# Attention row sums: inverse broadcast through DRAM in place of TensorE, and an earlier first transpose for short tiles

## The reference, cut to what matters

```python
s = jnp.einsum('bqhd,bkhd->bhqk', q[:, q0:kend], k[:, :kend]) * scale
s = s + c[:, :, q0:kend, None] - c[:, :, None, :kend]
p = jax.nn.softmax(jnp.where(mask[None, None], s, NEG_INF), axis=-1)
outs.append(jnp.einsum('bhqk,bkhd->bqhd', p, v[:, :kend]))
```

## Time and profile before

| what | value |
|---|---|
| median of three runs | 2929.63 us |
| the profiled execution (its span, the one time that the profile gives for it) | 2924.8 us |
| TensorE matmul busy | 2840.5 us, 97% |
| VectorE busy | 1712.9 us, 59% |
| ScalarE busy | 616.3 us, 21% |
| GpSimd busy | 1350.4 us, 46% |
| mean granted TensorE clock | 0.993 |

### The profile page before, as it was taken

The page is one execution under the profiler, slowest core; times in us unless marked ns, Lnnn a source line. Parts: engine busy times, 40 slices in busy tenths (PEclk is TensorE's granted clock), DMA queues, the critical chain, the costliest instruction groups (busy, mean ns, idle before and its releaser), DMA issues.

```text
span 2924.8 us, 40628 instructions
## 1 busy us (share of the span) xinstructions
PE 2840.5 (97%) x14442; PEld 2069.8 (71%) x14442; DVE 1712.9 (59%) x4617; ACT 616.3 (21%) x1269; POOL 1350.4 (46%) x1140
## 2 busy tenths in 40 slices
PE   8999999999999999998999989999999999999997
PEld 4478888888875555554455767878877777777775
DVE  6665656656346767674677534777677773332326
ACT  2221212110025454552110100011111111111114
POOL 3433534447730110101355335677667666555645
PEclk9999999999999999999999999999999999999999
DMA  6500110101121103014435456889989989999986
GB/s 219 184 6 1 31 45 1 30 15 44 30 77 35 63 30 129 28 33 170 173 137 159 131 198 197 270 277 277 271 277 289 291 271 302 305 304 305 317 258 254
DMA packets 192571, 470.49 MB, mean 161 GB/s; under 512 B 27384, under 2 KB 108104, under 8 KB 166632
## 3 DMA queue, kind: packets, MB, share of 16 engines
q1 hardware_dynamic: 145424, 347.63, 33.3%
q0 software_dynamic: 44640, 111.84, 16.5%
q10 hardware_dynamic: 2304, 8.39, 0.7%
HBM read 349.64 MB, written 118.11 MB: 160 GB/s over the span
## 4 chain that ended last, share of the span: by engine, by line
PE 39%; DMA 6%; DVE 3%; POOL 2%; issue 2%; SPq 1%; another core or an unknown queue 0%; ACT 0%; DVEq 0%; POOLq 0%; ACTq 0%
PE ps L3021 18%; PE ps L2796 6%; DMA moe_xg<-t_rows,index 5%; PE ps L2969 4%; PE ps L2940 3%; PE ps L2852 2%; DVE moe_xT L2097 2%; PE ps L2937 2%; POOL moe_xg L2523 1%; PE ps L2862 1%; PE ps L2815 1%; POOL moe_fin L2605 1%; PE ps L2806 0%; DMA base_rows<-moe_yo,index 0%
## 5 line engine op out<-in xcount | busy, mean ns | idle before, releaser
L2523 POOL DMA_INDIRECT moe_xg<-t_rows,index x433 | 428.6, 990 | 174.7 <-issue 139.2
L3021 PEld LDWEIGHTS ps<-moe_xT,moe_wg 128*128 128x128 f32 x2048 | 352.5, 196 | 54.6 <-issue 31.3
L3021 PE MATMUL ps<-moe_xT,moe_wg 128*128 128x192 f32 (+22 forms) x2048 | 380.0, 338 | 9.3 <-DVE moe_hh L1997 5.4
L3021 PE MATMUL ps<-moe_xT,moe_wu 128*128 128x192 f32 (+22 forms) x2048 | 376.3, 337 | 0.0
L3021 PEld LDWEIGHTS ps<-moe_xT,moe_wu 128*128 128x128 f32 x2048 | 354.2, 197 | 4.8
L2544 POOL DMA_INDIRECT base_rows<-moe_yo,index x100 | 231.0, 2310 | 273.2 <-DVE moe_yo L2111 116.8
L2097 DVE STREAM_TRANSPOSE moe_xT<-moe_xg 128x256 f32<-128x256 f32 x433 | 235.1, 610 | 174.2 <-DMA moe_xg<-t_rows,index 155.9
L1296 POOL TENSOR_TENSOR fox_diag<-fox_c,fox_causal 128x128 f32<-128x128 f32 x128 | 55.8, 457 | 450.9 <-DVE fox_mx L1325 446.1
L2660 ACT ACTIVATE moe_sl<-ps 128x256 f32<-128x256 f32 (+19 forms) x144 | 49.6, 345 | 953.9 <-PE ps L3021 736.8
L1997 DVE TENSOR_TENSOR moe_hh<-moe_sl,ps 128x256 f32<-128x256 f32 (+19 forms) x144 | 49.7, 358 | 292.4 <-ACT moe_sl L2660 194.9
L1319 DVE CUSTOM_DVE_ANT_0 hT<-ps,fox_c 128x512 f32<-128x512 f32 (+7 forms) x320 | 166.3, 560 | 63.0 <-PE ps L1581 62.7
(11 more groups left out here) (373 smaller groups left out, 5052.1 us busy)
## 6 DMA issues: line engine op xcount, KB each, us to landing
moe_wg<-in_we_gate SPq DMA_DIRECT2D x64, 1024.0 KB
moe_wu<-in_we_up SPq DMA_DIRECT2D x64, 1024.0 KB
moe_wd<-in_we_down SPq DMA_DIRECT2D x64, 1024.0 KB
fox_c<-ck SPq DMA_DIRECT2D x8, 1032.0 KB, 8.9
emb_xin<-in_x SPq DMA_DIRECT2D x16, 512.0 KB, 3.9
h_rows<-emb_hr SPq DMA_DIRECT2D x16, 512.0 KB, 2.7
ret_w<-in_w_in SPq DMA_DIRECT2D x16, 512.0 KB, 6.6
moe_yt<-h_rows SPq DMA_DIRECT2D x16, 512.0 KB
```

Source lines behind the costliest of these rows:

```text
L2523: pool.indirect_dma_start(out=xg[g % NXG][:, :], out_offset=None, in_=quarters, in_offset=bass.IndirectOffsetOnAxis(ap=route.index4[:, AT4 ...
L3021: ins = pe.matmul(out, w[:, c, f:FF:FC], xT[u][:, c, 0:n], start=(c == 0), stop=(c == DC - 1))
```

## The change

What it does, part by part:

1. `scatter` and its ones matrix are gone, as are the four diagonal matrices of `inverse` and the PSUM copy `keep`.
2. In their place SyncE runs `inverse_rows(n)`: it waits for the reciprocal, stores the 128 x 4 values to a small DRAM buffer, transposed (r outside, query inside, single elements of 4 bytes), waits for that store to land, and loads them back twice, once per head, broadcast over 64 partitions, into `rB` (256 columns).
3. `finish(n)` on VectorE now waits for the weighing of the whole tile and for both loads.
4. The store of tile n - 1 to `foxT` is issued after `inverse_rows(n)`, and the loads of pair p + 1 come after the store of the last tile of pair p - 1, in the middle of tile 8 (16) in place of its beginning.
5. `early` holds for t > 0 in place of t > 2, so for t = 2 and t = 1 too. For t = 1 the first two score chunks of tile n + 2 move with the transposes, in front of the last weighing.

```diff
-        onesf = sb("onesf", [P, FD])
-        rd = [sb(f"rd{b}", [P, 4, P]) for b in range(2)]
+            def inverse_rows(n):
+                b = n % 2
+                sp.wait_ge(inverted, n + 1)
+                sp.dma_start(rinv_rows[b].rearrange("r k -> k r"), rinv[b][:, :], allow_slow_non_contiguous=True).then_inc(rinv_out, 16)
+                sp.wait_ge(rinv_out, 16 * (n + 1))
+                if n >= 2:
+                    sp.wait_ge(scaled, n - 1)
+                for a in range(2):
+                    sp.dma_start(rB[b][FD * a:FD * (a + 1), :].rearrange("p (q k) -> p q k", q=2),
+                                 rinv_rows[b].rearrange("(q a) k -> a q k", a=2)[a].partition_broadcast(FD)).then_inc(rB_in[b], 16)
+
+            def store(n):
+                p, t = order[n]
+                sp.wait_ge(scaled, n + 1)
+                sp.dma_start(foxT[2 * FD * p:2 * FD * (p + 1), QT * t:QT * (t + 1)], oT[n % 2][:, :]).then_inc(o_s[n % 2], 16)
+
             for n, (p, t) in enumerate(order):
+                inverse_rows(n)
                 if n in TURN_AT:
...
-                sp.wait_ge(scaled, n + 1)
-                sp.dma_start(foxT[2 * FD * p:2 * FD * (p + 1), QT * t:QT * (t + 1)], oT[n % 2][:, :]).then_inc(o_s[n % 2], 16)
-                if (n + 1) % TILES == 0 and p + 2 < PAIRS:
-                    pair_values(p + 2)
-                    pair_gates(p + 2)
+                if n >= 1:
+                    store(n - 1)
+                if n >= 1 and n % TILES == 0 and p + 1 < PAIRS:
+                    pair_values(p + 1)
+                    pair_gates(p + 1)
+            store(NT - 1)
...
-                    dve.wait_ge(spread, n - 1)
+                    dve.wait_ge(rinv_out, 16 * (n - 1))
                 dve.reciprocal(rinv[b][:, :], rs[b][:, :]).then_inc(inverted, 1)
-                dve.wait_ge(inverted, n + 1)
-                for r in range(4):
-                    ins = dve.tensor_scalar(rd[b][:, r, :], ident[:, :], rinv[b][:, r:r + 1], None, ALU.mult)
-                ins.then_inc(rd_set, 1)
...
-                dve.wait_ge(spread_c, n + 1)
+                dve.wait_ge(weighed, step0[n + 1])
+                dve.wait_ge(rB_in[b], 32 * (n // 2 + 1))
...
-            def keep(n):
...
-            def scatter(n):
...
-                early = rounds > lead[n] and order[n][1] > 2
+                early = rounds > lead[n] and order[n][1] > 0
+                ahead_of = range(first[n + 2]) if n + 2 < NT and order[n][1] else []
...
                     if early and i == rounds - 1:
+                        for u in ahead_of:
+                            scores(n + 2, u)
                         for s in after:
                             turn(n + 1, s)
...
-                if early:
-                    scatter(n)
-                else:
-                    if order[n][1] == 0:
-                        for s in after:
-                            turn(n + 1, s)
-                        scatter(n)
-                    else:
-                        scatter(n)
-                        for u in (range(first[n + 2]) if n + 2 < NT else []):
-                            scores(n + 2, u)
-                        for s in after:
-                            turn(n + 1, s)
+                if not early:
+                    for u in ahead_of:
+                        scores(n + 2, u)
+                    for s in after:
+                        turn(n + 1, s)
```

More of the change, by code:

```diff
@@ L1104, in retention_phase, with fox_phase @@
         yield
-def fox_phase(nc, ps, ident, hT, square, w_in, w_out, v_rows, ck, mixed, mT_rows, foxT, ahead):
+def fox_phase(nc, ps, ident, hT, square, w_in, w_out, v_rows, ck, mixed, mT_rows, foxT, rinv_rows, ahead):
     with Phase(nc, "fox") as ph:
@@ L1190, in fox_phase @@
         zero = lambda name: ph.zero_sems(name, 1)[0]
-        tab, ones_set = ahead.fox_tab, zero("ones_set")
+        tab = ahead.fox_tab
         w_s, v_s, c_s = ahead.fox_w, ahead.fox_v, ahead.fox_c
@@ L1203, in fox_phase @@
         turned, pT_a, pT_d, weighed = (zero(n) for n in ("turned", "pT_a", "pT_d", "weighed"))
-        inverted, rd_set, spread, spread_c, scaled = (zero(n) for n in ("inverted", "rd_set", "spread", "spread_c", "scaled"))
+        inverted, rinv_out, scaled = (zero(n) for n in ("inverted", "rinv_out", "scaled"))
+        rB_in = ph.zero_sems("rB_in", 2)
         block = yield
@@ L1284, in _ @@
                     fox_token_sum(pool, ahead, hT, g, part)
-            pool.memset(onesf[:, :], 1.0).then_inc(ones_set, 1)
             pool.wait_ge(tab, 16)
@@ L1516, in _ @@
                         exps(n + 1, q, a)
-                    if i == 0 and n >= 1:
-                        keep(n - 1)
-            keep(NT - 1)
         @block.tensor
@@ L3075, in build @@
     mixed, foxT = dram("mixed", (SEQ, RH * RD)), dram("foxT", (FH * FD, SEQ))
-    mT_rows = dram("mT_rows", (NX, P, RH * P))
+    mT_rows, rinv_rows = dram("mT_rows", (NX, P, RH * P)), dram("rinv_rows", (2, 4, P))
     t_rows, base_rows = dram("t_rows", (SEQ + SPARE, D)), dram("base_rows", (SEQ + SPARE, D))
@@ L3086, in build @@
                   retention_phase(nc, ps, ident, hT, a["square"], a["w_in"], a["retc"], v_rows, ck, mixed, ahead),
-                  fox_phase(nc, ps, ident, hT, a["square"], a["w_in"], a["w_out"], v_rows, ck, mixed, mT_rows, foxT, ahead)]
+                  fox_phase(nc, ps, ident, hT, a["square"], a["w_in"], a["w_out"], v_rows, ck, mixed, mT_rows, foxT, rinv_rows, ahead)]
         for stage in stages:
```

## The result

The changed kernel takes 2960.74 us (median of 4 runs, 2959.97 to 2971.22), the kernel before 2928.45 (4 runs, 2926.21 to 2930.67). The ratio is 1.0114, with a 95% interval from 1.0094 to 1.0134: 32.3 us more, outside the range.

The account below looks back on a forecast made before the run. It took TensorE to set the pace in the attention stretch. Gains of 8.2 + 1.2 = 9.4 us by the last tile, less 1.1 us at the end, gave 2929.6 - 8.3 = 2921.3 us, range 2917 to 2928.5.

Parts of the forecast that it names:

- The failed step: SyncE's store of the inverse sums to DRAM, 512 pieces of 4 bytes: lands in 2.3 us, bounds 1.9 and 10.2.
- the chain: Reciprocal to `rB` through DRAM: store 2.3, loads 0.4 + 2.0, three handovers of 0.05, 4.9 us; ends 4.0 and 21.
- Rival B: Expensive 4-byte store: the chain outlasts its cover and VectorE stops in `finish`; at 15 us, 2939; chance 0.06.
- SyncE's work, off the path while it lands before `finish`: The added way through DRAM: hidden in 31 tiles at 4.9 us, with 8 us over; shortest cover 13.1 us.
- Moved on SyncE: Stores and loads queued behind `inverse_rows`, and small transfers behind bulk loads, still arrive in time: cost nothing.
- rival A: The scatter's gain is taken up by longer waits in following rounds: 2928.5 to 2930.7, say 2929; chance 0.19.
- The 20 long transitions: Tiles t = 7 to 3: removing the scatter gains 0.41 us of 0.54 at each, 8.2 us.
- t = 2 and t = 1: Short-tile transitions: gain 0 at t = 2, where TensorE waits for ScalarE; 0.4 us at three t = 1, 1.2 us.
- t = 0: Four transitions where TensorE waits 0.49 us for VectorE's copy: removing the scatter lengthens the wait, gain 0.
- Rival D: Earlier transposes at t = 1 and 2 hold up a ready weighing: up to 0.3 us in seven places, 2923.4; chance 0.08.
- VectorE's diagonals: Removing 28.0 us of diagonal matrices on VectorE gains nothing, as they never stand before the copy releasing TensorE.
- The end of the stage: Last tile, without cover: `finish` and everything behind the barrier come 1.1 us later, from 0.2 to 17 by the bounds.

Follow-up runs that it names:

- experiment 3: Changed kernel with the inverse sums stored as 128 side-by-side pieces of 16 bytes, wrong output: 2922.63 us, ratio 0.9978 to the kernel before.
- 5: Changed kernel with the same 512 4-byte stores, each word 64 bytes apart, wrong output: 458.40 us from first to last reciprocal; total 3204.68 us not comparable.
- experiment 4: Changed kernel with no store or loads of the inverse sums, `rB` filled once, wrong output: 2919.4 us, ratio 0.9972 to the kernel before.
- experiment 10: Changed kernel with TensorE transposing the sums, four 512-byte rows stored, scatter in the last two tiles, old short-tile order: 2917.89 us, ratio 0.9966 to the kernel before.
- experiment 7: Kernel before with only the new order for t = 2 and t = 1, scatter kept: 2917.35 us against 2914.11, ratio 1.0009.
- 9: Changed kernel with TensorE transposing the sums, four 512-byte rows stored, scatter in the last two tiles, new order: 2909.1 us against 2914.11, ratio 0.9978.
- experiment 1: Not the kernel: single small SyncE transfers, each waited for before the next; the changed kernel's store took 9.5 to 10.1 us from issue to issue.

## Why the prediction was wrong

**The failed step** is one term of the chain: "First transfer: 2 KB, but 512 pieces of 4 bytes; I take 2.3, near the small store, with bounds 1.9 and 10.2." It measured 8.2 us for the first, 8.5 in the median and up to 16 behind bulk loads. The upper bound held the first two; the choice "near the small store" was wrong, because the store of the earlier trace rows writes pieces of 1 KB, and this one writes 16 single words into each 64 bytes, from 16 partitions. With one block in place of single words (3) the term is 1.4 us for the first and 1.9 in the median, with the same 512 single words 64 bytes apart (5) 2.5 in the median, and in both the stalls in the middle are gone.

For this step the prediction cites the Trainium skill's "DMA: Bandwidth & Descriptors", which has one descriptor per element for a non-contiguous last dimension ("Rules for kernel authors") and a read-modify-write below 512 bytes ("Specifications"). Both hold for the fast layouts as well as for the slow one, and 512 elements of 4 bytes land in 1.9 us when 16 words apart, so neither tells the two apart. Whether a read-modify-write is what makes neighbours slow no run shows.

**The rest of the chain** was nearly right: one load alone takes 2.6 to 2.9 us with its issue, and the two together 3.4 us from the first issue to `finish` in the last tile (2.4 taken). With the store in one block the last `finish` comes 5.75 us behind the reciprocal, where 4.9 was forecast.

**Rival B** was the mechanism and its chance of 0.06 too small. But its pricing was off as well: at a chain of 12 us (8.5 + 3.4 and the handovers) it gives about 2928 (7.1 us more at the end than forecast), and 2961 was measured. Three parts were missing. First, "SyncE's work, off the path while it lands before `finish`" looked at one tile; SyncE waits 9 us per tile for the landing, and in that time neither the store for the next tile nor anything else is issued. In the last two tiles the landings add up: 20.56 us in place of 12. Second, "Moved on SyncE" comes to "Nothing": the retention rows come late (11.1 us in seven waits), and tiles 19 and 20 pay, where the small transfer stands behind 4 MB. With a landing of 2 us "nothing" is right, as experiment 3 shows; the two errors are one. Third, the clock: it halved in the 6.3 us stall of tile 20.

**Its sums.** Two are a little off besides: the gain is used up at a chain of 13.2 us, not 12.9 (1.1 + 8.3 = 9.4), and rival A begins at 2927.6, not 2928.5 (a third of 9.4, less 1.1). The range ended at 2928.5, although the prediction's own bounds for the end went to 17 us.

The Trainium skill's "DMA: Bandwidth & Descriptors", section "Queues, rings and completion order", has it that an issuing engine's queue is one ring on each of the same 16 DMA engines, and that each of them takes its descriptors in ring order. The 9.8 us of the store in one block behind 3 MB, against 1.4 alone, agree.

**The gains of TensorE.** Forecast 9.4 us by the last reciprocal, measured 7.6 in 3, 4, 5 and 10.

- *The 20 long transitions*: 0.41 us each forecast, 0.32 measured (tile periods 21.33 to 21.01, 18.87 to 18.55, 16.01 to 15.69, 13.11 to 12.79 and 10.91 to 10.59, each the same in every undisturbed kernel): 6.4 instead of 8.2. The timeline of the changed kernel at the transition of the earlier trace rows:

```profile
954.18 1.04 PE L1604 MATMUL ps<-ident,hT 128*16 128x128 f32 x8 [0.76 <-ACT hT L1489]
...
955.15 0.44 PE L1629 MATMUL ps<-fox_pT,fox_v 128*64 128x128 f32 x4
955.26 0.69 DVE L1366 COPY fox_pT<-ps 128x512 f32<-128x512 f32 x1 [2.54 <-PE ps L1604]
955.52 1.20 PE L1604 MATMUL ps<-ident,hT 128*128 128x128 f32 x8
```

Step 2 starts 0.37 us behind the last weighing (0.3 to 0.4 forecast, 0.81 before). Then steps 2 and 3 take 1.20 us together instead of 1.09, which is 0.11 in the copy's wait: of 0.44 us won 0.33 is left. The mechanism is the one forecast: step 3's first matmul, first row, starts 0.14 us behind the end of VectorE's copy and 0.94 behind the last weighing (0.95 forecast). What was off is its start before, second row:

```profile
956.09 0.30 PE L1604 MATMUL ps<-ident,hT 128*128 128x128 f32 x1
955.20 0.38 PE L1600 MATMUL ps<-ident,hT 128*128 128x128 f32 x2
```

The prediction took 955.26, half of the 1.09 us behind 954.71; but the matmuls overlap, so half of a row's length is more than the distance of its starts.

- *t = 2 and t = 1*: 0 + 0.4 forecast for what lies in the period of the t = 0 tile; it is 0.65 (8.23 to 7.58). The wait for ScalarE at t = 2 is 1.50 us, where "about 0.8" was to show it: most of the 0.81 us that is gone in front of that wait came back in it. *t = 0*: 0 forecast, and the period of the t = 7 tile behind it grows by 0.3 (33.43 to 33.73). VectorE's bias for the longest tile is the bound there; TensorE arrives sooner and waits longer (the first row is the changed kernel's, against 0.49 us of idle time before):

```profile
986.08 1.22 PE L1609 MATMUL ps<-ident,hT 128*128 128x128 f32 x8 [1.08 <-DVE fox_pT L1366]
```

Rival A is right in this one place: part of what is won at t = 1 is given back at the next t = 7. Net it is 0.35 us in each of three pairs, near the 0.4. Rival D's cost exists as well, but smaller than its price: the new order alone costs a net 0.4 us at a change of pair (experiment 7), and with the scatter gone it is neutral (experiment 10 has the same 7.6 us without it).

- *VectorE's diagonals* at nothing: right for the tile periods, since 3 and 4 gain no more than the scatter's share.

**The end of the stage**: +1.1 us forecast. In experiment 3, where the chain is as forecast, the end costs 1.8; in the changed kernel 16.6. **The sum** by the forecast's own method would be -7.6 + 1.8 = -5.8, which is what experiment 3's stage shows (468.43 - 474.24). Its runs have -5.9, but with other work possible behind the stage that agreement proves little.

## What to carry to other kernels

A chain through DRAM is priced by its address pattern, not by its bytes: ask of each store whether neighbouring words are written one by one, from one partition each, and if so transpose on chip first and store long rows. (A store in one block that is read back with a stride of 4-byte elements was not run.) Where that transpose stands counts too: in 9 and 10 it stood at the end of the tile and used up the cover in the t = 2 tiles; an earlier place was not run. A queue that waits for a landing in order, one wait per tile, has to be summed over everything behind it: the next store, the prefetches, and the last short tiles, where the cover ends. Where the trace lacks the row for an operation and the bounds are five times apart, the chance of the upper end is not small.

## What the hardware showed

- 4-byte stores from 128 partitions to neighbouring DRAM words land in 7.4 to 10.7 us, whether 128, 256 or 512 of them; 2 words apart in 3.6 to 4.4, 4 apart in 2.8, from 8 apart in 1.8 to 2.0 (2.1 to 2.8 in experiment 1, where each partition's four elements follow one another); into SBUF in 2.0. In the slow layout as in the fast one the DMA engines are through with the packets 1.3 us after the issue. That separate writes close together in DRAM wait for each other behind the engines is the reading that fits all of these; how large a line is, and which unit makes them wait, no run shows.
- The granted clock fell to 0.50 during the 6.3 us for which TensorE stood in mid-stage. It was 0.54 in the last tile of experiment 4, with TensorE idle 1.90 us before it, but 1.00 in the same place in experiment 3, with the same 1.90 us. What decides between these two was not found; from the transpose behind that wait to the last matmul it is 5.3 us in the one and 3.2 in the other.
